# Two attentions whose product of probabilities and values goes a head at a time, 512 query columns wide

## The reference, cut to what matters

```python
def _memory_cross_attention(h, mem_h, w_q, w_kv, q_norm_g, k_norm_g, w_o):
    ...
    logits = jnp.einsum('bhqd,bhkd->bhqk', q, mk).astype(jnp.float32) * (XA_HD ** -0.5)
    p = jax.nn.softmax(logits, axis=-1)
    o = jnp.einsum('bhqk,bhkd->bhqd', p, mv.astype(jnp.float32))
    return _merge_heads(o).astype(h.dtype) @ w_o

def _dilated_branch(q, k, v, rel_bias, window, dil):
    ...
    p = jnp.exp(logits - m[..., None])
    den = jnp.sum(p, axis=-1)
    num = jnp.einsum('bhrnqk,bhrnkd->bhrnqd', p, vb.astype(jnp.float32))
```

## Time and profile before

| | |
|---|---|
| median of 3 runs | 3112.32 us (3112.22 to 3112.53) |
| profiled execution, its own time | 3112.32 us |
| its span, first to last instruction | 3110.4 us |
| TensorE busy | 3088.4 us, 99% |
| VectorE busy | 1569.6 us, 50% |
| ScalarE busy | 1077.8 us, 35% |
| chain that ended last | TensorE 91%, VectorE 5%, ScalarE 2% |

### The profile page before, as it was taken

One profiled execution on the slowest core, in us unless ns is written; L12 is line 12 of the kernel. 1 busy time (PEld: TensorE's weight loads), 2 busy tenths in 40 slices (PEclk: granted clock), 3 DMA queues, 4 the chain that ended last, 5 costly groups with the idle time before them and its releaser, 6 DMA issues.

```text
span 3110.4 us, 36981 instructions
## 1 busy us (share of the span) xinstructions
PE 3088.4 (99%) x15460; PEld 2585.6 (83%) x15460; DVE 1569.6 (50%) x1899; ACT 1077.8 (35%) x1185; POOL 237.5 (8%) x139
## 2 busy tenths in 40 slices
PE   9999999999999999999999999999999999999999
PEld 7798988888889798888888778888888878888887
DVE  7564545554335554555435764544434766444432
ACT  3323344443233433344323332333323332333321
POOL 0002100010000010011001000101100000100100
PEclk9999999999999999999999999999999999999999
DMA  4412412222331131222323122222222322222222
GB/s 171 115 55 70 147 55 82 103 99 100 116 110 68 55 136 55 95 94 94 108 107 104 68 86 105 95 95 94 94 109 89 96 82 95 95 95 99 92 106 95
DMA packets 47566, 297.71 MB, mean 96 GB/s; under 512 B 7075, under 2 KB 7331, under 8 KB 13396
## 3 DMA queue, kind: packets, MB, share of 16 engines
q1 hardware_dynamic: 42336, 285.91, 25.9%
q10 hardware_dynamic: 5108, 10.02, 1.4%
HBM read 291.16 MB, written 4.75 MB: 95 GB/s over the span
## 4 chain that ended last, share of the span: by engine, by line
PE 91%; DVE 5%; ACT 2%; issue 1%; DMA 0%; POOL 0%; DVEq 0%; ACTq 0%; SPq 0%
PE G L461 84%; DVE wL L1703 1%; ACT wH L1261 1%; DVE mxt L1941 1%; PE psS L822 1%; PE psS L1023 1%; PE psS L1140 0%; PE G L1149 0%; PE G L1030 0%; PE psT L558 0%; DVE ws L2502 0%; PE psT L1176 0%; PE G L1064 0%; ACT ws L1361 0%; DVE ws L2315 0%
## 5 line engine op out<-in xcount | busy, mean ns | idle before, releaser
L461 PE MATMUL G<-hH,wH 128*128 128x512 f32 x2560 | 1016.4, 397 | 8.3 <-DVE wL L1703 3.3
L461 PE MATMUL G<-hH,wL 128*128 128x512 f32 x2560 | 999.5, 390 | 0.0
L461 PE MATMUL G<-hL,wH 128*128 128x512 f32 x2560 | 998.9, 390 | 0.0
L1703 DVE TENSOR_TENSOR wL<-raw,wH 128x2048 fp32r<-128x2048 f32 x260 | 626.5, 2409 | 635.6 <-ACT wH L1261 635.4
L461 PE MATMUL G<-wsr,wH 128*128 128x512 f32 (+1 forms) x2512 | 744.8, 380 | 1.3 <-DVE wsr L2331 0.9
L1261 ACT ACTIVATE wH<-raw 128x2048 fp32r<-128x2048 f32 x263 | 501.9, 1908 | 586.5 <-PE G L461 567.5
L461 PEld LDWEIGHTS G<-hH,wH 128*128 128x128 f32 x2560 | 482.0, 188 | 122.7 <-issue 20.3
L461 PEld LDWEIGHTS G<-hH,wL 128*128 128x128 f32 x2560 | 481.8, 188 | 102.8
L461 PEld LDWEIGHTS G<-hL,wH 128*128 128x128 f32 x2560 | 482.3, 188 | 98.5 <-issue 1.2
L461 PEld LDWEIGHTS G<-wsr,wH 128*128 128x128 f32 x2512 | 463.5, 188 | 91.8 <-DVE wsr L2331 1.8
L461 PE MATMUL G<-wsr,wL 128*128 128x512 f32 (+1 forms) x1256 | 475.8, 379 | 0.0
(11 more groups left out here) (296 smaller groups left out, 2511.1 us busy)
## 6 DMA issues: line engine op xcount, KB each, us to landing
raw<-in_units SPq DMA_DIRECT2D x263, 1024.0 KB, 4.8
ws<-bias_rows SPq DMA_DIRECT2D x2, 1536.0 KB, 15.1
bias_rows<-ws ACTq DMA_DIRECT2D x1, 2560.0 KB
x<-in_x SPq DMA_DIRECT2D x4, 512.0 KB, 7.6
ws<-in_mem ACTq DMA_DIRECT2D x2, 1024.0 KB, 4.9
ws<-bias_rows ACTq DMA_DIRECT2D x1, 2048.0 KB, 8.6
out_x<-x SPq DMA_DIRECT2D x3, 512.0 KB, 7.3
ws<-in_decay ACTq DMA_DIRECT2D x1, 1280.0 KB, 7.8
```

The lines of the kernel that those rows point to most:

```text
L461: mm = pe.matmul(o, mv if swap else wt, wt if swap else mv, start=first and n == 0, stop=last and n == 2)
L1703: V.tensor_tensor(wL[:, g.p, :], raw[:, g.p, :], wH[:, g.p, :].bitcast(F32), ALU.subtract)\
```

## The change

The PV product no longer goes with every row. In both attentions it waits for the last row of a head and is done for the whole head. In the memory attention that is four matmuls of 512 columns in place of sixteen of 128. In the dilated attention it is one matmul for each block of 128 keys, over the queries from that block on (512, 384, 256 and 128 columns, added up in one bank) in place of ten of 128. Only the last head is cut in two: rows 0 to 2 at the last step but one, and row 3 in the last step. The number of products is the same; the order of the other instructions, on every engine, is too.

```diff
@@ attention(), the memory attention's steps
                     r = s_ - PV_LAG
                     if r >= 0:
-                        pe.wait_ge(pt_ready, c.row.v + (r + 1))
-                        if r == 0:
-                            pe.wait_ge(ms_ready, keys_read + 4)
-                        if r % (ST * per_job) == 0:
-                            take_job()
-                        mm = pv(r // ST, r % ST)
-                        if r % (ST * per_job) == ST * per_job - 1:
-                            end_job(mm)
+                        upto = r % ST + 1
+                        if upto == ST or (r == rows - 2 and upto == ST - 1):
+                            pe.wait_ge(pt_ready, c.row.v + (r + 1))
+                            if r == ST - 1:
+                                pe.wait_ge(ms_ready, keys_read + 4)
+                            first = ST - 1 if r == rows - 1 else 0
+                            if first == 0:
+                                take_job()
+                            mm = pv(r // ST, first, upto)
+                            if upto == ST:
+                                end_job(mm)
@@ the dilated attention's steps
-                            for kt in range(qt + 1):
-                                mm = pe.matmul(G[:, 1 + 2 * (h % 2), qt * P:qt * P + P], ov[:, kt, h * P:h * P + P],
-                                               opt[:, h % 2, kt, qt * P:qt * P + P], start=(kt == 0), stop=(kt == qt))
+                            if qt == ST - 1 or r == 30:
+                                pe.wait_ge(pt_ready, c.row.v + (r + 1))
+                                first = ST - 1 if r == 31 else 0
...
+                                for kt in range(qt + 1):
+                                    q0, q1 = max(first, kt) * P, (qt + 1) * P
+                                    mm = pe.matmul(G[:, 1 + 2 * (h % 2), q0:q1], ov[:, kt, h * P:h * P + P],
+                                                   opt[:, h % 2, kt, q0:q1], start=(kt == 0), stop=(kt == qt),
+                                                   skip_group_check=True)
@@ pv() of the memory attention
-                            mm = pe.matmul(G[:, c.job.p * 2 + t, qt * P:qt * P + P],
+                            mm = pe.matmul(G[:, c.job.p * 2 + t, q0 * P:q1 * P],
                                            xv[:, kt, h * 256 + t * P:h * 256 + t * P + P],
-                                           xpt[:, h % 2, kt, qt * P:qt * P + P], start=(kt == 0), stop=(kt == 1))
+                                           xpt[:, h % 2, kt, q0 * P:q1 * P], start=(kt == 0), stop=(kt == 1))
```

More of the change, by code:

```diff
@@ L977, in _ @@
                             h, qt = r // ST, r % ST
[L978 to L983, removed]
-                            for kt in range(qt + 1):
-                                mm = pe.matmul(G[:, 1 + 2 * (h % 2), qt * P:qt * P + P], ov[:, kt, h * P:h * P + P],
-                                               opt[:, h % 2, kt, qt * P:qt * P + P], start=(kt == 0), stop=(kt == qt))
-                            if qt == ST - 1:
-                                mm.then_inc(pv_done, 1)
+                            if qt == ST - 1 or r == 30:
+                                pe.wait_ge(pt_ready, c.row.v + (r + 1))
+                                first = ST - 1 if r == 31 else 0
+                                if first == 0:
+                                    pe.wait_ge(job_free, values + 2 + 2 * (h // 2))
+                                    if h > 1:
+                                        pe.wait_ge(pv_free, c.pv.v + h - 1)
+                                for kt in range(qt + 1):
[3 more added lines that the diff above has]
+                                                   skip_group_check=True)
+                                if qt == ST - 1:
+                                    mm.then_inc(pv_done, 1)
                     c.row.off += 32
@@ L1025, in score, with pv @@
                     return mm
-                def pv(h, qt):
+                def pv(h, q0, q1):
                     for t in range(2):
                         for kt in range(2):
-                            mm = pe.matmul(G[:, c.job.p * 2 + t, qt * P:qt * P + P],
+                            mm = pe.matmul(G[:, c.job.p * 2 + t, q0 * P:q1 * P],
                                            xv[:, kt, h * 256 + t * P:h * 256 + t * P + P],
-                                           xpt[:, h % 2, kt, qt * P:qt * P + P], start=(kt == 0), stop=(kt == 1))
+                                           xpt[:, h % 2, kt, q0 * P:q1 * P], start=(kt == 0), stop=(kt == 1))
                     return mm
```

## The result

The changed kernel takes 3133.15 us (median of 6 runs, 3132.82 to 3134.33) against 3112.3 us before: a ratio of 1.0069, 95% interval 1.0058 to 1.0079, so 0.7% slower. The forecast of the likeliest case was 3127.2, the range 3119 to 3134. The profiled execution took 3133.55 us, its span is 3131.7.

A forecast was written before the change was run, and what follows sets the result against it. The prediction took the attentions to be bound almost equally by TensorE and the softmax chain on ScalarE and VectorE. It added 11.5 us (memory) and 3.4 (dilated), +14.9 in all, to 3112.3 for 3127.2 us, range 3119 to 3134.

The forecast's parts named there:

- the likeliest case: Whole kernel: delays of 11.5 us in the memory attentions and 3.4 in the dilated one, 3127.2 us; chance 0.78.
- What the wide matmuls save: PV products of all three attentions: wide matmuls save 0.5 us twice and 0.6, in all 1.6 us of TensorE.
- The memory attention: Each memory attention: TensorE waits on the ScalarE-VectorE chain, PV work comes later; +5.75 us each, 11.5 for two.
- The two stretches: Memory attention, score 9 to 12 and score 13 to its transposes: chain stays 6.32 and 6.52 us, each costing 2.7.
- The small terms: Memory attention: score 8 waits 0.35 us, the last piece costs 0.5, and the wide matmuls save 0.5.
- The dilated attention: Dilated attention: longer PV pieces delay the scores that VectorE needs; +3.4 us in all, bounds -0.6 to +8.8.
- The shares of the heads: Dilated attention: +0.8 us at head 3, +1.2 at head 4, +0.9 at head 5, +0.5 at the end.
- The clock: Rival: a granted-clock fall behind each of four new memory-attention waits, 4 x 1.7 = 6.8 us more, 3134; chance 0.08.
- a sign of being wrong: Memory attentions' new waits: wrong if under 1 us, if head copies start earlier, or if the granted clock falls behind them.
- the long pieces repay the waits: Rival: ScalarE and VectorE work ahead beside long pieces, TensorE stays the bound; 3110.7 or 3109.4 us; chance 0.04.
- Wide passes at fp32r speed: Rival: wide float32 records take an fp32r record's 0.23 us, saving 18 us over the attentions, 3109; chance 0.02.
- Only half is lost: Rival: VectorE's order leaves room or the dilated attention hides its share; delay 5 to 6 us, 3118; chance 0.08.

The follow-up runs named there:

- narrow: Changed kernel's order, a head at a time, but products in matmuls of 128 columns as before: 3136.45 us (before 3112.5; ratio 1.0076).
- late_copy_memory: Changed kernel with the memory attentions' head splits (heads 0 and 1) three steps later on ScalarE and VectorE: 3120.5 us (before 3111.93; ratio 1.0029).
- pairs_memory: Kernel before, with the memory attentions' product two rows at a time, 256 columns wide, last two rows singly: 3117.57 us (before 3111.93; ratio 1.0017).
- after: The changed kernel itself, against the kernel before: 3133.15 us (before 3112.3; ratio 1.0069).
- busy_dilated: Product by heads only in the dilated attention, plus five unused 512-column matmuls in TensorE's waits: 3115.42 us (before 3111.5; ratio 1.0011).
- memory_only: Changed kernel with the dilated attention's old code, only the two memory attentions by heads: 3128.35 us (before 3112.5; ratio 1.005).
- late_copy_rows: Memory attentions by heads with head splits three steps later, dilated one row by row as before: 3114.69 us (before 3111.5; ratio 1.001).

## Why the prediction was right, and by how much it was not

*What the wide matmuls save.* Right in the turns: a wide record's is 0.43 us, four narrow ones take 0.45. Of the 1.6 us reckoned from them, 1.1 show in the stages of `narrow`.

*The memory attention.* Right in mechanism and size. The two stretches came out at 6.25 and 6.52 us against 6.32 and 6.52 read from the trace of before; the waits are 2.47 and 2.75. Without clock an attention costs 9.0 - 3.4 = 5.6 and 7.3 - 1.7 = 5.6 us, and 5.7 with the waits filled, where 5.75 was reckoned. The small terms came out a little lower: the last piece was 0.4 us late, not 0.5 (transposes at 448.14, four turns of 0.11, the piece at 448.99), and score 8 waited 0.25, not 0.35. `late_copy_memory` and `pairs_memory` show by two other ways that it is the head split in the chain, met by less work for TensorE.

*The dilated attention.* The sum of 3.4 us is what `after` and `busy_dilated` have. VectorE was 0.88 us late behind head 4 where 0.9 was reckoned. The shares of the heads came out otherwise. By the starts of VectorE's bias additions (L2315, L2322 after), counted from the first of them, the changed kernel is level up to row 12, 1.04 us late at row 13 (behind head 1) and 0.77 at rows 22 to 24, 1.73 at row 25 (behind head 4) and 2.68 at row 29 (behind head 5). So the terms are 0.8, as reckoned, 0.95 where 1.2 was reckoned, 0.95 for 0.9, and 0.7 for the 0.5 of the end. Two errors of 0.2 cancel, and that the sum is right to a tenth is partly luck. VectorE did not wait behind every long piece either, but by 1.95 (0.89 before), 0.88 and 0.87 us behind heads 1, 4 and 5, and by under 0.1 behind heads 0, 2 and 3.

*Sum and forecast.* The likeliest case was off by 6 us, and the step that failed is "The clock", not the sum of 14.9: 21.3 us are 5.6 + 5.6 + 3.4 from the chain, 14.6, and four clock stretches of 1.7, 6.8, less 0.2 and rounding. The forecast put the clock at nothing, and named as a sign of being wrong that the granted clock falls behind the new waits: it did, behind three of the four. That rival named 3134 us, and had a chance of 0.08. I took as evidence against it that a wait of 1.4 us in the kernel before had no fall behind it, but that was one wait half as long as the new ones. The same trace has a nearer row at the start of the kernel, a wait of 2.25 us with the clock down behind it, and I did not use it:

```profile
10.01 0.79 PE L461 MATMUL G<-hH,wH 128*128 128x512 f32 x1 [2.25 <-DVE wL L2051]
...
10.00:13.40 3.40, 3.39 (x8) 2.72 (x9) 2.96 (x4) 3.40 (x6) 0.00 (x0) 0.50 1.04 434
```

(Even this row would not have decided it: behind the same wait, of 2.17 us, the clock stays up in `memory_only`.) Moreover the wait of 1.4 us does have a fall behind it in another execution, that of `late_copy_rows`, whose dilated code is that of before. The rival was not right in its places either. Three of the four stretches lie behind new long waits, one long wait (ahead of 1227 in the second memory attention) has none, and the fourth is behind the dilated attention, where it comes with the old code as well. So that the rival's time of 3134 was met to 1 us is in part luck. The Trainium skill (TensorE: Matmul & The Clock Gate, Why this matters for your kernels) warns of idle gaps between bursts of matmuls, but of longer ones than stand here; in these traces the clock fell behind waits of 2.47, 2.75 and 1.93 us already, so the measurement goes further than the rule.

*The rivals.* That the long pieces repay the waits fell: in the long piece of 3.6 us nothing was made up, 47.5 and 49.2 us say so. Wide passes at fp32r speed fell by the 0.43. "Only half is lost" fell as well: the chain alone took 14.6 us.

What stays open: what sets whether a wait of 1 to 3 us is followed by a fall of the clock, and why the stretch behind the dilated attention is single in some runs and double in others. Four waits of 1.8 us had none, one of 0.87 with 0.82 behind it had one, and waits in the same code had it in one execution and not in another. Each stretch moves a kernel's time by 1.7 us, so a difference of 2 or 3 us between two of these runs says little without the trace.

## What to carry to other kernels

Where two engines work in turn, small matmuls between the steps may be there to fill the time of the other engine's chain. Before gathering them into fewer, wider ones, measure from the trace how long the chain takes between two of this engine's steps, and what is left to do in it: the difference is a wait, and the gathered work comes on top. Move with it what hangs on its end (here the head split), and keep TensorE from standing still for microseconds: behind nine of twelve waits of 2.5 to 2.75 us its clock fell, and the next matmuls paid a second time.

## What the runs showed of the hardware that I had not expected

- Matmuls whose output nobody reads made the kernel faster: six of 0.86 us in each memory attention, -4.9 us in all; five in the dilated one, -2.4 to -3.4 (by which kernel before they are set against).
- The long piece behind a wait of 2.75 us took 5.29 in place of 3.60 us.
- A single-precision matmul of 512 columns costs 3.8 times one of 128 in turns (0.43 against 0.112 a record), so that for float32 operands width gains almost nothing here.
